# Cross-attention of a streaming encoder: values as three rounded products, scores ahead of the turns, VectorE's steps in another order

## The reference, cut to what matters

```python
def _mem_attn(h, mk, mv, w_q, q_norm, w_o):
    q = _rmsnorm((h @ w_q).reshape(bsz, t, X_HEADS, X_HEAD_DIM), q_norm)      # 4 heads of 256
    logits = jnp.einsum("bthd,bmhd->bhtm", q, mk) * (X_HEAD_DIM ** -0.5)
    probs = jax.nn.softmax(logits, axis=-1)
    o = jnp.einsum("bhtm,bmhd->bthd", probs, mv).reshape(bsz, t, X_HEADS * X_HEAD_DIM)
    return o @ w_o
```

## Time and profile before

| | us |
|---|---|
| median of 3 runs | 1684.48 (1682.56 to 1684.67) |
| the profiled execution, whole | 1682.37 |
| its span | 1680.6 |
| TensorE busy | 1595.6 (95%) |
| VectorE busy | 997.4 (59%) |
| ScalarE busy | 636.5 (38%) |
| GpSimd busy | 635.8 (38%) |

### The profile page before, as it was taken

How to read it: one execution, slowest core, us unless ns; L and a number is a source line. 1 busy time by engine, 2 the same in 40 slices (tenths; PEclk the granted TensorE clock), 3 DMA queues, 4 the chain that set the end, 5 groups by cost and what they waited for, 6 DMA issues and landing times.

```text
span 1680.6 us, 31053 instructions
## 1 busy us (share of the span) xinstructions
PE 1595.6 (95%) x11888; PEld 1511.4 (90%) x11890; DVE 997.4 (59%) x1416; ACT 636.5 (38%) x960; POOL 635.8 (38%) x303
## 2 busy tenths in 40 slices
PE   5889987999999999999999979999899999999999
PEld 5789853998699999999999979799699999999999
DVE  5899966456355555455656879556646555045530
ACT  4333356335333333233333665443524333133320
POOL 2235550232043334333434644733124334333332
PEclk9999999999899999999999989999999999999999
DMA  4333330124032222222222322324012223222222
GB/s 170 118 114 112 103 114 1 63 76 163 1 113 81 86 92 100 69 88 87 100 88 91 104 82 84 131 89 175 26 51 77 86 87 103 85 76 87 87 104 89
DMA packets 41714, 153.46 MB, mean 91 GB/s; under 512 B 5344, under 2 KB 5856, under 8 KB 40360
## 3 DMA queue, kind: packets, MB, share of 16 engines
q1 hardware_dynamic: 41640, 152.42, 26.4%
HBM read 145.20 MB, written 9.30 MB: 92 GB/s over the span
## 4 chain that ended last, share of the span: by engine, by line
PE 73%; issue 10%; POOL 6%; DVE 5%; ACT 4%; DMA 0%; POOLq 0%; DVEq 0%; SPq 0%; ACTq 0%
PE PS L831 66%; POOL WLO L411 6%; PE AX L1100 2%; DVE TB L1595 1%; DVE RSTD L1215 1%; ACT WHI L442 1%; PE AX L1010 1%; DVE RB L1597 1%; PE AX L1106 1%; PE AX L1038 1%; PE AX L894 1%; PE PS L1021 1%; ACT LG L626 1%; DVE RB L1599 0%; PE PS L1072 0%
## 5 line engine op out<-in xcount | busy, mean ns | idle before, releaser
L411 POOL TENSOR_TENSOR WLO<-WRAW,WHI 128x1024 fp32r<-128x1024 f32 (+3 forms) x299 | 635.6, 2135 | 1029.5 <-ACT WHI L442 1029.3
L442 ACT ACTIVATE WHI<-WRAW 128x1024 fp32r<-128x1024 f32 (+3 forms) x299 | 268.7, 918 | 690.9 <-PE PS L831 636.5
L831 PE MATMUL PS<-XH,WHI 128*128 128x272 f32 (+1 forms) x2256 | 475.7, 292 | 26.6 <-POOL WLO L411 18.2
L831 PE MATMUL PS<-XH,WLO 128*128 128x272 f32 (+1 forms) x2256 | 469.4, 290 | 0.0
L831 PE MATMUL PS<-XL,WHI 128*128 128x272 f32 (+1 forms) x2256 | 467.1, 289 | 0.0
L831 PEld LDWEIGHTS PS<-XH,WHI 128*128 128x128 f32 x2256 | 360.9, 190 | 34.8 <-POOL WLO L411 17.8
L831 PEld LDWEIGHTS PS<-XL,WHI 128*128 128x128 f32 x2256 | 360.2, 190 | 0.0
L831 PEld LDWEIGHTS PS<-XH,WLO 128*128 128x128 f32 x2256 | 358.4, 190 | 0.0
L831 PE MATMUL PS<-HH,WHI 128*128 128x272 f32 x1216 | 253.0, 289 | 0.7 <-DVE HL L1448 0.7
L831 PE MATMUL PS<-HL,WHI 128*128 128x272 f32 x1216 | 251.8, 288 | 0.0
L831 PE MATMUL PS<-HH,WLO 128*128 128x272 f32 x1216 | 251.8, 288 | 0.0
(11 more groups left out here) (239 smaller groups left out, 1628.1 us busy)
## 6 DMA issues: line engine op xcount, KB each, us to landing
WRAW<-in_w_in_even SPq DMA_DIRECT2D x29, 512.0 KB, 3.5
WRAW<-in_w_up0a SPq DMA_DIRECT2D x22, 512.0 KB, 3.4
WRAW<-in_w_up0b SPq DMA_DIRECT2D x22, 512.0 KB, 3.4
WRAW<-in_w_up1a SPq DMA_DIRECT2D x22, 512.0 KB, 3.4
WRAW<-in_w_up1b SPq DMA_DIRECT2D x22, 512.0 KB, 3.4
WRAW<-in_w_mv SPq DMA_DIRECT2D x16, 512.0 KB, 3.5
WRAW<-in_w_xq SPq DMA_DIRECT2D x16, 512.0 KB, 3.4
WRAW<-in_w_xo SPq DMA_DIRECT2D x16, 512.0 KB, 3.4
```

The lines of the kernel that those rows point to most:

```text
L411: pool.tensor_tensor(WLO[parity][:, first:last], WRAW[parity][:, first:last], WHIf[parity][:, first:last], ALU.subtract).then_inc(lo_done, ...
L442: act.activation(WHI[parity][:, first:last], WRAW[parity][:, first:last], ACT.Copy).then_inc(hi_done, 2 // len(cuts))
L831: ins = pe.matmul(dst, w, x, start=first, stop=last)
```

## The change

It computes the values of the prompt's units as three rounded products. For that, ScalarE rounds MV to MVH and VectorE subtracts to MVL, which lies where MV lay (so it waits until the store of MV has landed), and each turned unit is kept as a high part PTH (ScalarE) and a low part PTL (VectorE, `turn_low`). The stores of MK and MV are issued ahead of the loads of the query weights. scores(1) waits for chunk 6 alone, scores(2) for chunk 7. TensorE's order behind chunk 7 becomes scores(1), head_mean(3), scores(2), turn(0), values(0), turn(1), scores(3), values(1), turn(2), scores(4), values(2), turn(3), values(3), turn(4), values(4). head_std(3) moves ahead of exponentials(1). VectorE does query_head(2) ahead of the eviction of chunk 7, and its steps behind that are reordered. The sample's values stay F32, with their own buffer PTX.

```diff
@@ -217,7 +217,12 @@
 
         QX = at("QX", [P, 8, T], F32, S2)
         PX0, PX1 = at("PX0", [P, 4, MEM], F32, HTAIL), at("PX1", [P, 4, MEM], F32, LTAIL)
-        PTX = at("PTX", [P, 2, 2, 512], F32, XHL_AT)
+        PTH, PTL = pack(XHL_AT, HHL_AT, [("PTH", [P, 2, 2, 512], F32R), ("PTL", [P, 2, 2, 512], F32R)])
+        PTHf = PTH[:].bitcast(F32)
+        PTX = at("PTX", [P, 256], F32, XHL_AT + 16384)
+        MVH = at("MVH", [P, 2, D], F32R, S2 + 8 * T * 4)
+        MVL = at("MVL", [P, 2, D], F32R, M_AT + 8192)
+        assert S2 + 8 * T * 4 + 8192 <= END
 
         GB, YB, GE, H32 = pack(S2, END, [("GB", [P, 4 + TG], F32), ("YB", [P, TG], F32), ("GE", [P, TG], F32),
                                          ("H32", [P, T], F32)])
@@ -272,6 +277,7 @@
 
         xs_done, xnm, xexp, xp, xt_done = sem("xs_done"), sem("xnm"), sem("xexp"), sem("xp"), sem("xt_done")
         xt_read, xpv_done, xyh, xyl = sem("xt_read"), sem("xpv_done"), sem("xyh"), sem("xyl")
+        mvh_ready, mvl_ready, xt_low = sem("mvh_ready"), sem("mvl_ready"), sem("xt_low")
 
         gb_ready, gconv0, gconv, gelu_done = sem("gb_ready"), sem("gconv0"), sem("gconv"), sem("gelu_done")
         hh_ready, hl_ready = sem("hh_ready"), sem("hl_ready")
@@ -296,6 +302,11 @@
             return ap.rearrange("p (h n) -> p h n", h=2)
 
         LEN = {p[0]: p[1] for p in PHASES}
+        assert T0["xq0"] % 2 == T0["xq1"] % 2 == 1
+
+        def low_turns(l, s):
+
+            return 4 * l + sum(u < 4 for u in XUNITS[0:s])
 
         def odd_key_mean(p):
 
@@ -371,16 +382,16 @@
                     stream("out_odd")
                     n += store(o["c_state"], CSTATE[:])
                     n += store(o["h_last"], HST[:])
-                stream(f"xq{l}")
-
-
-                sp.wait_ge(*((yl_even, A_TILES + 5) if l == 0 else (chunk_done, C0["out_odd"])))
-                sp.dma_start(CK[:], a["cache_mk"][l]).then_inc(cache_landed, 16)
-                sp.dma_start(CV[:], a["cache_mv"][l]).then_inc(cache_landed, 16)
                 sp.wait_ge(*((hn_out, HN0["mk0"] + 4) if l == 0 else (k1_out, 2)))
                 n += store(o["mem_k"][l], MK[:])
                 sp.wait_ge(evicted, T0[f"mv{l}"] + 2)
                 n += store(o["mem_v"][l], MV[:])
+                stream(f"xq{l}")
+
+
+                sp.wait_ge(*((yl_even, A_TILES + 5) if l == 0 else (chunk_done, C0["out_odd"])))
+                sp.dma_start(CK[:], a["cache_mk"][l]).then_inc(cache_landed, 16)
+                sp.dma_start(CV[:], a["cache_mv"][l]).then_inc(cache_landed, 16)
                 stream(f"xo{l}")
                 if l == 0:
 
@@ -651,11 +662,16 @@
                 for hd in range(XHEADS):
                     ahead(c0 + 2 * hd + 1)
                     head_square(u0 + hd, QX[:, 2 * hd:2 * hd + 2, :], t0 + 2 * hd + 2)
+                    if hd == 1:
+                        act.wait_ge(evicted, T0[f"mv{l}"] + 2)
+                        for mb in range(2):
+                            act.activation(MVH[:, mb, :], MV[:, mb, :], ACT.Copy).then_inc(mvh_ready, 1)
                     if hd == 2:
                         exponentials(0)
                     if hd < XHEADS - 1:
                         ahead(c0 + 2 * hd + 2)
                         head_std(u0 + hd, False)
+                head_std(u0 + XHEADS - 1, False)
                 for s in range(1, 7):
                     if s < 5:
                         exponentials(s)
@@ -665,11 +681,9 @@
                         if v >= 2:
                             act.wait_ge(xpv_done, b + v - 1)
                         if XUNITS[v] < 4:
-                            act.activation(PTX[:, v % 2, :, :], AX[:, 0:2, :], ACT.Copy).then_inc(xt_read, 1)
+                            act.activation(PTH[:, v % 2, :, :], AX[:, 0:2, :], ACT.Copy).then_inc(xt_read, 1)
                         else:
-                            act.activation(PTX[:, v % 2, 0, 0:256], AX[:, 0, 0:256], ACT.Copy).then_inc(xt_read, 1)
-                    if s == 1:
-                        head_std(u0 + XHEADS - 1, False)
+                            act.activation(PTX[:], AX[:, 0, 0:256], ACT.Copy).then_inc(xt_read, 1)
                     if s >= 2:
                         v, u = s - 2, XUNITS[s - 2]
                         act.wait_ge(xpv_done, b + v + 1)
@@ -1055,8 +1069,8 @@
                     u = XUNITS[s]
                     if s == 0 and l:
                         pe.wait_ge(xyl, b)
-                    if s == 1:
-                        pe.wait_ge(evicted, t0 + 8)
+                    if s in (1, 2):
+                        pe.wait_ge(evicted, t0 + 6 + s)
                     if s >= 3:
                         pe.wait_ge(xexp, 4 * (b + s) - 4)
                     pe.wait_ge(hn_out, u0 + min(u, 3) + 1)
@@ -1078,8 +1092,9 @@
                     pe.wait_ge(xp, b + s + 1)
                     if s:
                         pe.wait_ge(xt_read, b + s)
-                    if s < 2:
-                        pe.wait_ge(hn_std, u0 + 3 + s)
+                        pe.wait_ge(xt_low, low_turns(l, s))
+                    else:
+                        pe.wait_ge(hn_std, u0 + XHEADS)
                     for i in range(4):
                         for mb in range(2):
                             if XUNITS[s] < 4:
@@ -1095,16 +1110,19 @@
                     if s or l:
                         pe.wait_ge(xyl, b + s)
                     if u < 4:
+                        pe.wait_ge(mvl_ready, 2 * l + 2)
+                        pe.wait_ge(xt_low, low_turns(l, s + 1))
                         for d in range(2):
+                            w = slice(P * (2 * u + d), P * (2 * u + d) + P)
                             for mb in range(2):
-                                ins = pe.matmul(AX[:, 2 + d, :], MV[:, mb, P * (2 * u + d):P * (2 * u + d) + P],
-                                                PTX[:, s % 2, mb, :], start=mb == 0, stop=mb == 1)
+                                ins = product([AX[:, 2 + d, :]], MVH[:, mb, w], MVL[:, mb, w], [PTH[:, s % 2, mb, :]],
+                                              [PTL[:, s % 2, mb, :]], mb == 0, mb == 1)
                     else:
                         for m in range(8):
                             for mb in range(2):
                                 at_ = 32 * (2 * (m // 2) + mb)
                                 ins = pe.matmul(AX[:, 2, 32 * m:32 * m + 32], CV[:, mb, P * m:P * m + P],
-                                                PTX[:, s % 2, 0, at_:at_ + 32], start=mb == 0, stop=mb == 1)
+                                                PTX[:, at_:at_ + 32], start=mb == 0, stop=mb == 1)
                     ins.then_inc(xpv_done, 1)
 
                 for m in range(8):
@@ -1117,18 +1135,19 @@
                         scores(0)
 
                 scores(1)
+                head_mean(u0 + XHEADS - 1)
+                scores(2)
                 turn(0)
-                scores(2)
-                pe.wait_ge(xt_read, b + 1)
-                head_mean(u0 + 3)
                 values(0)
                 turn(1)
-                for s in range(3, 5):
-                    scores(s)
-                    turn(s - 1)
-                    values(s - 2)
+                scores(3)
+                values(1)
+                turn(2)
+                scores(4)
+                values(2)
+                turn(3)
+                values(3)
                 turn(4)
-                values(3)
                 values(4)
 
                 linear(f"xo{l}", KT, HH, HL, xyl, [b + 4] * 6 + [b + 5] * 2)
@@ -1502,28 +1521,46 @@
                         dve.tensor_tensor(HL[:, 0:8, SS:T], AX[:, 2, 0:256].rearrange("p (m q) -> p m q", q=SAMPLE),
                                           HHf[:, 0:8, SS:T], ALU.subtract).then_inc(xyl, 1)
 
+                def values_low(mb):
+                    dve.wait_ge(mvh_ready, 2 * l + mb + 1)
+                    dve.wait_ge(out_stored, 16 * (8, 13)[l])
+                    dve.tensor_tensor(MVL[:, mb, :], MV[:, mb, :], MVH[:].bitcast(F32)[:, mb, :], ALU.subtract).then_inc(mvl_ready, 1)
+
+                def turn_low(s):
+                    if XUNITS[s] < 4:
+                        dve.wait_ge(xt_read, b + s + 1)
+                        if s >= 2:
+                            dve.wait_ge(xpv_done, b + s - 1)
+                        dve.tensor_tensor(PTL[:, s % 2, :, :], AX[:, 0:2, :], PTHf[:, s % 2, :, :], ALU.subtract).then_inc(xt_low, 1)
+
                 for hd in range(XHEADS):
                     evict(c0 + 2 * hd, t0 + 2 * hd, (t0 + 2 * hd) % 2, QX[:, 2 * hd, :])
                     if hd == 3:
                         normalise(0)
-                    elif hd:
+                    if hd:
                         query_head(hd - 1)
                     evict(c0 + 2 * hd + 1, t0 + 2 * hd + 1, (t0 + 1) % 2, QX[:, 2 * hd + 1, :])
-                    if hd == 3:
-                        query_head(2)
                     head_sum(u0 + hd, T)
                     if hd == 2:
```

(30 more changed lines are left out.)

## The result

The changed kernel takes 1692.13 us (median of five, 1691.64 to 1693.89) against 1684.33 for the kernel before (1682.56 to 1684.67, now also of five): ratio 1.0052, 95% interval 1.0038 to 1.0065, so it is slower, by half a per cent. The forecast was 1692.0. The profiled execution took 1692.69, with a span of 1690.9.

A forecast was written before the change was run, and what follows sets the result against it. TensorE, 95% busy, was taken to bound the kernel, with slack in the cross-attention tails. Two tails of 51.4 us, 102.8 - 95.4 = +7.4 us, on 1684.48 gave 1692; range 1684 to 1698.

The forecast's parts named there:

- A: Cross-attention tail behind values(3) grows by a serial chain at half clock: +7.4 us, about 1692; chance 0.52.
- Products at 0.235 us, 2.8 us a step: Prompt-unit values: 12 rounded products replace eight 0.43 us records, 0.62 us less a step, -5.0 us TensorE work at full clock.
- The last eviction and head 3's mean: Tail start: scores(1) skips the last eviction's wait, starting 0.8 us sooner; head_mean(3) waits until 408.0.
- rival C: Clock falls in earlier thin stretches, slowing scores(3): +1.7 us a layer, about 1695.5; chance 0.20.
- The values(3) step: Last third of the tail: values(3) takes 5.2 us, between 4.98 and 5.38 seen before.
- full-clock walk: Step-by-step count of the tail at full clock: 48.1 us after the projection's end, +0.8 us over both layers.
- The chain: Between values(3) and values(4): turn(4), copy, turn_low and sample's low part, 3.9 us, plus 0.95 at half clock.
- The sum of a tail: Query projection's end to output projection's first matmul: 51.4 us in each layer, 102.8 together against 95.4.
- MVH and MVL at nothing: Value copies and subtractions fall in idle times of the query projection: cost nothing; without that cover 2.5 us a layer.
- E, the stores: Stores delay the query weights, 1 to 3 us a layer on top of A: up to 1698; chance 0.05.
- B, faster: Copy and subtraction stay beside TensorE's work in the tail, which sets the pace: 1678; chance 0.13.
- D, full clock: A's order in the tail, but the clock does not fall: +0.8 us, 1685; chance 0.10.

The follow-up runs named there:

- warm: Changed kernel plus unread 512-column matmuls in TensorE's waits (10 ahead of scores(3), 12 ahead of values(3), 12 ahead of values(4)): 1683.13 us, 1.0002.
- before_warm: Kernel before plus one unread F32 matmul ahead of each of turn(4), values(3) and values(4): 1677.26 us, 0.9959.
- stores_alone: Kernel before with only the stores of memory keys and values moved ahead of the query weights' loads: 1684.56 us, 1.0006.
- before_turn4_late: Kernel before with only turn(4) moved behind values(3): 1690.21 us, 1.0032.
- turn4_first: Changed kernel with only turn(4) put back ahead of values(3) on TensorE: 1684.07 us, 0.9993.
- head3_early: turn4_first with VectorE's query_head(3) and maximum(3), and TensorE's scores(3) and scores(4), moved earlier: 1688.57 us, 1.0023.
- early_warm: head3_early plus unread matmuls in waits, with values rounded ahead of the next turn's copy and low_part(1) ahead of turn_low(2): 1675.34 us, 0.9955 against the kernel before.

## Why the prediction was right

The forecast was A, 1692.0, with +7.4 us; the medians say +7.8, the profiled pair's tails +10.0. By its own steps:

- **Products at 0.235 us, 2.8 us a step.** Measured 2.87 (416.50 to 419.37), in starts 0.235 apart. The Trainium skill, TensorE: Matmul & The Clock Gate, section "Back-to-back issue gap", has N/2.4 + 2.5 ns, 216 ns for 512 columns, for a single matmul's gap; the trace does not agree, and its 0.235 decided rightly. For the half clock the same section of the Trainium skill has N/1.2, 427 ns, and there the trace agrees: 452.67 to 456.08 is 8 starts of 0.426.
- **The last eviction and head 3's mean.** scores(1) without its 0.82 us of waiting, head_mean at 408.5 for a forecast of 408.0, with the projection's end 0.35 later.
- **values(0) at 416.0 with the projection's end at 403.7**: 12.3 us. Measured 416.50 - 404.05 = 12.45. **scores(3)** 18.6: measured 18.71, after 2.35 us of waiting (forecast 2.5).
- **values(3)** 36.3: 36.18 in layer 1, 37.62 in layer 0. The difference is rival C, which did happen there: the clock is half from 422.4 to 425.8, and scores(3) takes 5.04 us to the next start instead of 3.61. Forecast +1.7 where it occurs, measured 1.43, in one layer of two.
- **The values(3) step** is the one that was mis-sized, at 5.2 us. It was taken from two rows of before (4.98 and 5.38) as if half clock changed little. Both were partly at half clock. The true price is 3.54 us at full clock (warm) and 6.82 at half (after, layer 1), and in layer 0 it took 5.74. So the half clock costs this step 3.3 us, not 0.2, and the full-clock walk was too long by 1.5 a layer: it gave 48.1 us a tail, and warm measures 46.4.
- **The chain** from the end of values(3) to values(4): 3.9 + 0.95 = 4.85 forecast, 4.70 measured in both layers. At full clock its forecast was +2.9 against before; warm less before_warm has +2.65.
- **values(4)** 5.0: measured 4.87 and 4.79. The upper bound of 5.9 is the length of the F32 step in layer 0 of before; by the prediction's own 0.43 us a product, twelve cannot pass 5.1.
- **The granted clock** half from about 442 to 454: in layer 0 it was from 442.9 to 456.5. In layer 1 it fell earlier, in the wait ahead of values(3), at 1221.1, so that all of that step ran at half.
- **The sum of a tail** 51.4: measured 52.93 and 52.49. Of the 2.6 us too little, 1.4 are the clock's fall in layer 0 (which stood under C, not under A) and 2.2 the values(3) step (5.74 and 6.82 for 5.2 twice); the other terms give about 1 back. The medians show only +7.8, as the profiled execution of before was 2.0 us under its median (stores_alone shows how its clock can return later) and that of after 0.6 above. So the mechanism and the range were earned, but a median within 0.2 us of the forecast is luck.
- **MVH and MVL at nothing**: they are in idle time. In the timeline of DVE VectorE still waits 1.64 us behind them:

```profile
393.33 2.36 DVE L1527 TENSOR_TENSOR MVL<-MV,MVH 128x1024 fp32r<-128x1024 f32 x2
397.33 0.72 DVE L1240 TENSOR_TENSOR QX<-PS,RSTD 128x544 f32<-128x544 f32 x1 [1.64 <-PE PS L845]
```

- **E, the stores**: 0, as stores_alone shows. **B, faster**, fell by its own point: the gap ahead of values(4) is over 1 us and scores(3) waits. **D, full clock**, did not occur, but warm made it by hand: 1.0002 for a forecast of +0.8 us, which is 1.0005. In the tails warm has 92.9 us for D's 96.2, so this nearness is partly luck as well; most of the difference is the values(3) step.

A weighed its parts wrongly in one way. It counted +0.8 for the order at full clock and +6.6 for the clock. Against a kernel before that loses clock time too, warm and before_warm give the cleaner split: in the tails, 4.7 us for the order at full clock, and 5.3 us more clock loss than before (105.4 - 92.9 = 12.5 against 95.4 - 88.2 = 7.2).

## What to carry to other kernels

Where a step's output has to pass two other engines before the next step, do the step that feeds that chain first, and put work that is ready into the wait: one transpose group on the wrong side of values(3) cost 5.4 us by itself (before_turn4_late), and with it put right the rest of the change won nothing that shows (turn4_first, 0.9993). When an order is changed, look for what is late next in the engines that serve it: the same two operations in the other order on ScalarE and VectorE left a new wait of 3.55 us in head3_early, and with the half clock behind it the earlier scores won nothing. And price each step at either clock from rows at that clock; where TensorE waits behind short matmuls, a few unread 512-column matmuls in the gap can be the cheapest gain there is.

## What the runs showed of the hardware that was not expected

- The clock fell without a long idle time. In early_warm it was half from 442.3 to 445.7, though TensorE shows no idle time between 437 and 442.3; what it did there were 3 added matmuls, eight transposes and the 32-column matmuls of the sample. Busy time of two stretches:

```profile
440.00:442.00 2.00, 2.00 (x20) 2.00 (x20) 1.23 (x1) 0.00 (x0) 0.00 (x0) 1.00 0.04 8
442.00:444.00 2.00, 2.00 (x9) 1.81 (x9) 0.42 (x1) 0.38 (x1) 0.00 (x0) 0.57 0.00 0
```

- It is not the same from layer to layer: the same work ran scores(3) at 5.04 us to the next start in layer 0 of after and 3.61 in layer 1; in turn4_first it was the reverse (3.61 in layer 0, whose fall had come earlier, and 5.04 in layer 1). What in a stretch decides it was not settled by these runs.
- The 32-column F32 matmuls double with the clock (0.11 to 0.21 us each: 3.54 and 6.82 us for 32), and in early_warm the clock fell while they ran. A price for them from a row that is partly at half clock, as 4.98 and 5.38 were, fits neither.
- The added matmuls in idle gaps showed no cost of their own in the steps behind them: values(3) of warm starts 36.22 us behind the projection's end, and 36.18 without them.
